# An accumulating DMA in place of a VectorE subtraction for 68 weight slots of a two-model transformer kernel

## The reference

```
f = swiglu_ffn(rms_norm(h, norm_ffn_pre[layer]), w_ffn_in[layer], w_ffn_out[layer])   # layers a, b
h = h + rms_norm(f, norm_ffn_post[layer])
...
h = h + conv_ffn(rms_norm_2(h, ffn_norm[layer]), ...)                                  # layers c, d
    g, u = jnp.split(h @ w_ffn_in, 2, axis=-1)
    return (jax.nn.silu(g) * u) @ w_ffn_out
```

## Time and profile before

| | before |
|---|---|
| median of 2 runs | 2247.4 us (2247.08 to 2247.72) |
| span of the profiled execution, first to last instruction | 2245.6 us |
| TensorE matmul busy | 2227.9 us (99%) |
| TensorE weight load busy | 1943.6 us (87%) |
| VectorE busy | 1469.1 us (65%) |
| ScalarE busy | 1042.3 us (46%) |
| GpSimd busy | 3.7 us |
| DMA | 218.93 MB, 97 GB/s over the span |
| granted TensorE clock | 0.999 of full speed |

### The profile page before, as it was taken

One profiled execution on the slowest core, in us unless ns is written; L12 is line 12 of the kernel. 1 busy time (PEld: TensorE's weight loads), 2 busy tenths in 40 slices (PEclk: granted clock), 3 DMA queues, 4 the chain that ended last, 5 costly groups with the idle time before them and its releaser, 6 DMA issues.

```text
span 2245.6 us, 39159 instructions
## 1 busy us (share of the span) xinstructions
PE 2227.9 (99%) x15283; PEld 1943.6 (87%) x15283; DVE 1469.1 (65%) x2158; ACT 1042.3 (46%) x1635; POOL 3.7 (0%) x6
## 2 busy tenths in 40 slices
PE   9999999999999999999999999999999999999998
PEld 7788898989988988989988878899888888898888
DVE  7675767642877777662557665888843875888833
ACT  7455644432526644342432364544532784544622
POOL 0000000000000000000000000000000000000000
PEclk9999999999999999999999999999999999999999
DMA  4212232342462223332242112333232203232232
GB/s 168 74 61 93 94 110 95 102 125 85 133 204 88 92 97 103 103 101 97 87 118 77 58 48 93 95 103 103 96 102 94 78 29 112 95 112 93 95 102 85
DMA packets 82910, 218.93 MB, mean 97 GB/s; under 512 B 10976, under 2 KB 31840, under 8 KB 82784
## 3 DMA queue, kind: packets, MB, share of 16 engines
q1 hardware_dynamic: 74832, 207.68, 28.8%
q10 hardware_dynamic: 7952, 9.47, 1.4%
HBM read 212.78 MB, written 4.34 MB: 97 GB/s over the span
## 4 chain that ended last, share of the span: by engine, by line
PE 95%; DVE 2%; ACT 1%; DMA 1%; issue 1%; SPq 1%; DVEq 0%; ACTq 0%
PE bank L584 20%; PE bank L586 20%; PE bank L585 20%; PE bank L796 5%; PE bank L799 4%; PE bank L800 4%; PE bank L892 3%; PE bank L891 3%; PE bank L893 3%; PE bank L606 2%; PE bank L607 1%; PE bank L610 1%; PE bank L1081 1%; PE bank L1203 1%; DMA raw<-weights_dram 1%
## 5 line engine op out<-in xcount | busy, mean ns | idle before, releaser
L2130 DVE TENSOR_TENSOR w_lo<-raw,w_hi 128x1024 fp32r<-128x1024 f32 x344 | 419.3, 1222 | 337.8 <-ACT w_hi L1397 333.7
L1397 ACT ACTIVATE w_hi<-raw 128x1024 fp32r<-128x1024 f32 x344 | 361.5, 1056 | 483.1 <-PE bank L586 323.6
L584 PE MATMUL bank<-u_hi,w_hi 128*128 128x512 f32 (+1 forms) x1466 | 546.5, 373 | 2.5 <-ACT av L1776 1.2
L585 PE MATMUL bank<-u_lo,w_hi 128*128 128x512 f32 (+1 forms) x1466 | 542.1, 370 | 0.0
L586 PE MATMUL bank<-u_hi,w_lo 128*128 128x512 f32 (+1 forms) x1466 | 541.8, 370 | 0.0
L584 PEld LDWEIGHTS bank<-u_hi,w_hi 128*128 128x128 f32 x1466 | 275.2, 188 | 52.3 <-DVE u_lo L2165 2.3
L586 PEld LDWEIGHTS bank<-u_hi,w_lo 128*128 128x128 f32 x1466 | 275.2, 188 | 47.9
L585 PEld LDWEIGHTS bank<-u_lo,w_hi 128*128 128x128 f32 x1466 | 275.3, 188 | 46.6 <-issue 1.4
L584 PE MATMUL bank<-hid_hi,w_hi 128*128 (+1 forms) x440 | 171.4, 390 | 1.2 <-DVE w_lo L2130 1.2
L586 PE MATMUL bank<-hid_hi,w_lo 128*128 (+1 forms) x440 | 171.2, 389 | 0.0
L585 PE MATMUL bank<-hid_lo,w_hi 128*128 (+1 forms) x440 | 171.2, 389 | 0.0
(11 more groups left out here) (380 smaller groups left out, 4233.9 us busy)
## 6 DMA issues: line engine op xcount, KB each, us to landing
raw<-weights_dram SPq DMA_DIRECT2D x363, 512.0 KB, 3.5
bz<-gated_dram SPq DMA_DIRECT2D x30, 268.0 KB, 4.2
raw<-weights_dram ACTq DMA_DIRECT2D x13, 512.0 KB, 4.4
gated_dram<-bz SPq DMA_DIRECT2D x8, 274.0 KB, 4.5
h<-x_t_dram SPq DMA_DIRECT2D x8, 256.0 KB, 6.0
raw<-weights_dram SPq DMA_DIRECT2D x4, 256.0 KB, 5.2
out_dram<-m SPq DMA_DIRECT2D x4, 256.0 KB, 2.4
out_dram<-m ACTq DMA_DIRECT2D x4, 256.0 KB, 2.5
```

The lines of the kernel that those rows point to most:

```text
L584: pe.matmul(out, wh, xh, start=start, stop=False)
L585: pe.matmul(out, wh, xl, start=False, stop=False)
L1397: act.activation(slot_of(w_hi, s, i), slot_of(raw, s, i), ACT.Copy).then_inc(hi_ready, 1)
L2130: dve.tensor_tensor(slot_of(w_lo, s, i), slot_of(raw, s, i), slot_of(w_hi, s, i).bitcast(F32), ALU.subtract)\
```

## The change

For slots n = 5 to 21 of each of the four FFN outputs (17 slots each, 68 in all, `BY_DMA`), VectorE's subtraction is gone. ScalarE, right after the rounded copy `w_hi`, waits for its own copy and writes `w_lo = -w_hi` (a second activation of the same shape, scale -1). GpSimd waits for it (`neg_ready`) and issues a DMA that adds the slot's weights, read a second time from HBM, to `w_lo` in place. Its landing counts in `low_landed[s % 4]`, and TensorE waits on that for these slots, through the new helper `made`, which also renumbers `w_ready` for the others. The values are the same difference as before; the low part is no longer rounded by an engine on its way.

Some semaphores are merged to make room. In half 0 TensorE's loop over slots 1 to 8 is written out, since slots below 5 and above wait on different semaphores. VectorE's `way_back` keeps only the low parts of the next stage's slots.

```diff
+BY_DMA = tuple(SLOT[f"{l}_ffn_out"] + n for l in "abcd" for n in range(5, 2 * HALF))
+def made_before(s):
+    return s - sum(n < s for n in BY_DMA)
+def landed_of(s):
+    return sum(n <= s and n % RING == s % RING for n in BY_DMA)
...
-            pool.memset(bwv[:, :, :, :], 0.0).then_inc(taps_zeroed, 1)
+            pool.memset(bwv[:, :, :, :], 0.0).then_inc(pool_zeroed, 1)
+            for n, s in enumerate(BY_DMA):
+                pool.wait_ge(neg_ready, n + 1)
+                pool.dma_start(slot_of(w_lo, s), weights[s], accum_op=ALU.add).then_inc(low_landed[s % RING], 16)
...
+            def made(s, i=0):
+                if isinstance(i, int):
+                    s, i = s + RING * i, 0
+                if s in BY_DMA:
+                    pe.wait_ge(low_landed[s % RING], 16 * i + 16 * landed_of(s))
+                else:
+                    pe.wait_ge(w_ready, RING * i + made_before(s) + 1)
...
                     back(half, 0, first=True)
-                    with pe.Fori(0, 2) as i:
-                        for n in range(1, 1 + RING):
-                            back(half, n, i)
+                    if half:
+                        with pe.Fori(0, 2) as i:
+                            for n in range(1, 1 + RING):
+                                back(half, n, i)
+                    else:
+                        for n in range(1, 1 + 2 * RING):
+                            back(half, n)
...
                 act.activation(slot_of(w_hi, s, i), slot_of(raw, s, i), ACT.Copy).then_inc(hi_ready, 1)
+                if s in BY_DMA:
+                    act.wait_ge(hi_ready, s + RING * i + 1)
+                    act.activation(slot_of(w_lo, s, i), slot_of(w_hi, s, i).bitcast(F32), ACT.Copy, scale=-1.0).then_inc(neg_ready, 1)
...
             def low_part(s, i=0):
+                if s in BY_DMA:
+                    return
...
                 s = SLOT[f"{l}_ffn_out"] + HALF * half
-                if half == 0:
-                    for n in range(2, HALF - 1):
+                if half:
+                    for n in range(2 * RING, HALF - 1):
                         low_over(s + n)
-                    return
-                with dve.Fori(0, 2) as i:
-                    for n in range(RING):
-                        low_over(s + n, i)
-                for n in range(2 * RING, HALF - 1):
-                    low_over(s + n)
```

More of the change, by code:

```diff
@@ L304, in build @@
         hi_ready, w_ready, slot_done = sem("hi_ready"), sem("w_ready"), sem("slot_done")
+        neg_ready, low_landed = sem("neg_ready"), [sem(f"low_landed{j}") for j in range(RING)]
         x_landed = [sem(f"x_landed{c}") for c in range(KC)]
+        bz4_landed = x_landed[:CONV_RING]
         gain_landed, vec_landed, consts_landed, mask_landed, dist_landed = (sem(n) for n in (
@@ L325, in build @@
         gc_evac, gc_ready, z_ready, sconv = sem("gc_evac"), sem("gc_ready"), sem("z_ready"), sem("sconv")
-        qk_evac, qkh_ready, qkl_ready, f_evac, f_sum, c_high, c_low, zeroed, rounded, sel_ready, mask_zeroed = (sem(n) for n in ("qk_evac", "qkh_ready", "qkl_ready", "f_evac", "f_sum", "c_high", "c_low", "zeroed", "rounded", "sel_ready", "mask_zeroed"))
+        qk_evac, qkh_ready, qkl_ready, f_evac, f_sum, c_high, c_low, zeroed, rounded, sel_ready = (sem(n) for n in ("qk_evac", "qkh_ready", "qkl_ready", "f_evac", "f_sum", "c_high", "c_low", "zeroed", "rounded", "sel_ready"))
         tok_full, tok_ln, tok_ready = sem("tok_full"), sem("tok_ln"), sem("tok_ready")
@@ L331, in build @@
             "pt_full", "pt_ready", "o_ready", "oh_ready", "ol_ready"))
-        b_evac, b_sig, bz_ready, taps_zeroed, taps_landed, bw_ready, conv_full, conv_made = (sem(n) for n in (
-            "b_evac", "b_sig", "bz_ready", "taps_zeroed", "taps_landed", "bw_ready", "conv_full", "conv_made"))
+        b_evac, b_sig, bz_ready, pool_zeroed, taps_landed, bw_ready, conv_full, conv_made = (sem(n) for n in (
+            "b_evac", "b_sig", "bz_ready", "pool_zeroed", "taps_landed", "bw_ready", "conv_full", "conv_made"))
         mask_step, y_kept, spread_full = sem("mask_step"), sem("y_kept"), sem("spread_full")
         bz_kept = sem("bz_kept")
-        bz4_landed = [sem(f"bz4_landed{j}") for j in range(CONV_RING)]
         shift_full, shift_ready, b_sums, b_squares, mean_full, mean_ready, msq_ready, var_full, var_ready, xc_ready, yn_ready = (
@@ L523, in load_taps @@
             def load_taps():
-                sp.wait_ge(taps_zeroed, 1)
+                sp.wait_ge(pool_zeroed, 2)
                 for i in range(SHIFTS):
@@ L591, in chunk @@
             def chunk(s, i, out, xh, xl, ready=None, ks=range(KC)):
-                pe.wait_ge(w_ready, s + RING * i + 1)
+                made(s, i)
                 for k in ks:
@@ L607, in chunk_low_last @@
                     pe.matmul(out, weight(w_hi, s, k), xl[:, k, :], start=False, stop=False)
-                pe.wait_ge(w_ready, s + 1)
+                made(s)
                 for k in ks:
@@ L614, in two_chunks @@
             def two_chunks(s, outs, xh, xl, ready, ready_hi=None):
-                pe.wait_ge(w_ready, s + 2)
+                made(s + 1)
                 for k in range(KC):
@@ L634, in three_chunks @@
             def three_chunks(s, outs, xh, xl, ready_hi, ready_lo):
-                pe.wait_ge(w_ready, s + 3)
+                made(s + 2)
                 for k in range(KC - 1):
@@ L895, in back_half_by_half @@
                 def back_half_by_half(n):
-                    pe.wait_ge(w_ready, s1 + HALF + n + 1)
+                    made(s1 + HALF + n)
                     for half in range(2):
@@ L961, in _ @@
                 if k == 4:
-                    pe.wait_ge(w_ready, 2)
+                    made(1)
                 for s in range(2):
@@ L1327, in out_parts @@
                 pe.wait_ge(d_q_evac, KC)
-                pe.wait_ge(w_ready, SLOT["d_out"] + ns[-1] + 1)
+                made(SLOT["d_out"] + ns[-1])
                 for k in ks:
@@ L2644, in _ @@
                 if hd == 0:
-                    dve.wait_ge(mask_zeroed, 1)
+                    dve.wait_ge(pool_zeroed, 1)
                 after(dve, pt_full, 4 * hd)
```

12 lines of the change are left out of this document (6 added, 6 removed).

## The result

The changed kernel takes 2274.12 us, the median of 2 runs (2273.84 to 2274.4), against 2247.4 before. The ratio is 1.0121, with an interval of 1.0091 to 1.015: slower by 26.7 us. The forecast was 2267, slower by 19.8; the range of 2254 to 2298 holds the time.

What follows compares the result with a forecast made beforehand. TensorE, matmuls busy 99% of the span, was taken as the bound. Link minus slack at five places gave 18.3 us, plus 1.5 us for slot 21's loads: 19.8 us on 2247.4, forecast 2267 us, range 2254 to 2298.

Steps and rivals of the forecast that it cites:

- what the removed work is worth: 68 VectorE subtractions of 1.222 us, 83 us busy; TensorE waited for only one, so worth 0 us.
- ScalarE's second pass: One more activation of 1.056 us per slot, 72 us in all, where ScalarE waits anyway: 0 us.
- The link: From the negated copy's end through GpSimd's adding DMA to TensorE: 5.7 us, making each of 68 slots ready later.
- The short slacks: Ends of layers a, b, d and slot 13 of c, ready 1.8 to 4.0 us early: losses 3.9, 3.6, 3.4, 1.7 us.
- three half microseconds: 0.5 us each in three layers, for slot 21's load running beside slot 20's addition: 1.5 us.
- The steady slots: The other slots' low parts lie ready 8.6 us before TensorE takes them: loss 0.
- The tap place: Layer a, slot 8, whose load follows 16 tap issues: slack 0, loss 5.7 us; slots 9 and 10 no more.
- signs of being wrong: Link under 3 or over 8.6 us, negated copy much longer, `raw` loads slowed beside additions, or the clock dropping.
- the third rival: TensorE's clock falls to 1.2 GHz after each new wait, losing half its time: about 9 us, 2276 us; chance 0.15.
- The hidden link: Rival: the link is about 3.5 us and hidden except at the taps: losses 7.8 us, 2255 us; chance 0.12.
- A gain through VectorE: Rival: VectorE's freed 83 us speed some boundary that hangs on it: 2243 to 2247 us; chance 0.03.
- A stall at each slot: Rival: link over 8.6 us, TensorE waits at all 68 slots, one third of the excess each: 2303 to 2370 us; 0.15.

Runs made afterwards that it cites:

- x3: The changed kernel with VectorE subtracting again at the taps' slots and the short-slack ends, 49 slots left by DMA: 2245.24 us, ratio 0.9996 to the kernel before.
- x1: The changed kernel with VectorE subtracting again in slots 5 to 10 of layer a, 62 slots left by DMA: 2262.65 us, ratio 1.0076 to the kernel before.
- x12: The changed kernel run again with no edit, as reference for the other runs: 2274.44 us, ratio 1.0129 to the kernel before.
- x8: The changed kernel with VectorE subtracting again in slots 8 to 10 of layer a: 2267.46 us, ratio 1.0093 to the kernel before.
- x10: The changed kernel with 40 small matmuls on TensorE during the wait before slot 8 of layer a: 2271.5 us, ratio 1.0108 to the kernel before.
- x11: The kernel with DMA in 49 long-slack slots only, each addition held until the slot two before is done: 2339.98 us, ratio 1.0427 to the kernel before.
- x6: The changed kernel with GpSimd adding the weights twice and ScalarE writing -2 times `w_hi`: 2553.21 us, ratio 1.1365 to the kernel before.
- x9: The changed kernel with VectorE subtracting again in slots 5 to 7 of layer a: 2269.25 us, ratio 1.0098 to the kernel before.
- x4: The changed kernel with GpSimd's DMA copying the weights instead of adding them: 2262.68 us, ratio 1.0078 to the kernel before.
- x2: The changed kernel with VectorE subtracting again in slots 18 to 21 of layers a, b, d and slot 13 of c: 2259.15 us, ratio 1.0057.

## Why the prediction held, and where it was off

**What bounds, and what the removed work is worth.** Right. The subtractions gave 0: in `x3` 49 of them are gone and the interval is 0.9986 to 1.0005. The same number carries the written-out loop and ScalarE's second pass: with the removed work they change the time by 3 us at most.

**The link.** Forecast 5.7, measured 5.86 at layer a's slot 8. That the total is so near is partly luck, since the parts are others: I had 1.3 us fixed and 2 x 2.2 of moving; the runs show 0.3 us until the issue, 3.8 for a plain copy by this path and 1.6 more for the addition.

**The short slacks.** Right in place, and in size within 0.9 us each: 3.5, 4.5, 2.1 and 3.7 us, 13.8 in all, against 14.1 with the three half microseconds that were added. `x1` keeps just these and measured +15.7. The sum went by slot 21, whose excess is the largest; most of the wait stood at slot 20, with a slack of 3.05 (2.29 us idle in layer a), and slot 21 added 0.57. And layer b's 4.5 holds 1.5 us of a low clock, not of link. Without it the four ends cost 12.3 us, nearer to the 12.6 of the slacks alone: no run shows the 1.5 us that were added for slot 21's load, and that the total came out near 14.1 is luck.

**The steady slots.** Right away from the taps: no wait in any of the slots with 8.6 us, and `x3` has none. Beside the taps slot 7 of layer a waited 0.65 us (1.43 in `x12`): its addition, issued at 481.91, took 9.0 us to land, the longest of the 68.

**The tap place is the step that failed.** The prediction costs slot 8 at L alone, 5.7, and says that the additions of slots 6 and 7 beside the taps "are in the range, not in the sum". They belonged in the sum: 4.7 us by the start of slot 8's copy in the change; `x8` against `x1` gives 5.3, with a low clock in it. The reason was written beside it, queues that are up to 0.88 busy. What I did not follow was who is behind them: the additions lengthen SyncE's 16 issues, SyncE issues in order, and the load of slot 8, already the latest thing in the kernel, stands behind the sixteenth. At a place with no slack every microsecond of crowding counts in full. Of the prediction's own signs of being wrong, two were seen, this late load and the falling clock.

**The clock, the third rival,** was partly true, and it lay on top of the sum as it said. It fell at slot 8 and cost 2.8 us there (`x10` takes it away), and in layer b in one of two executions of the change; in the same two it held after waits of 1.7 to 2.3 us and once after 2.75. I had priced half of each wait, 9 us; the windows of the first execution give 4.3. The Trainium skill (TensorE: Matmul & The Clock Gate, section "Part 1: The HAM clock gate (the "warmup" mystery)") has an idle array fall to half rate; the 0.50 behind the longest wait agrees.

With both, the forecast's 19.8 becomes 19.8 + 4.7 + 2.8 = 27.3 us, near the measured 26.7 and 28.1. (The sum leaves out layer b's 1.5 us of clock, and carries the 1.5 us for slot 21 that no run shows; they cancel.)

**The other rivals.** The hidden link, 2255 us, fell with the 5.4 us to landing. A gain through VectorE did not show in `x3`. A stall at each slot did not occur in the change, since 5.86 is under 8.6; how near that is to the edge is seen in `x11`, where a landing of 7.7 us under a shorter slack costs 93.7 us.

## What to carry to other kernels

Before a step of a buffer's preparation is moved to a DMA, list for each use how long the prepared buffer lies ready, and compare with the new link. Here the places where it was shorter, and the traffic beside one of them, made the whole bill, and leaving just these out of the change brought the loss to zero; if the engine that is relieved was not the bound, zero is also the best to hope for. Where the queues are crowded at the place with no slack, follow the issuing engine's order: what counts is the load behind the crowd, and it goes into the sum.

## What the runs showed of the hardware

- An accumulating DMA of 512 KB from HBM onto SBUF, issued by GpSimd, landed in 5.4 us (5.1 to 9.0 over 68), a plain one by the same path in 3.8, and SyncE's in 3.3. A slot's first addition beside the second of the slot ahead took 8.8 (median, `x6`), and issued together with a load 7.7 (`x11`).
- Sixteen small DMA issues on SyncE's queue took 10.3 us alone, 13.0 beside GpSimd's plain copies, and 14.9 to 16.1 beside its additions (seven profiles). One queue's issues can be slowed by another's traffic.
- The granted clock was 0.50 after each idle time of 3.96 us (`x8`), 7.0 (`x9`), 8.1 (`x4`), 9.9 (the change), 10.1 (`x2`) and 11.3 us (`x12`). Of the 21 idle times from 1.98 to 3.44 us counted above it fell to 0.50 after 12 and stayed at 1.00 after nine. Small matmuls in place of the idle time kept it at 1.00 (`x10`).
